# Gate and value projections of a 4-mixer block: two more weight sums on GpSimd, another product order behind the seam, modulation turns moved

## The reference, cut to what matters

```python
def swiglu(u, w1, w3, w2):
    return (jax.nn.silu(u @ w1) * (u @ w3)) @ w2
...
for l in range(DEPTH):                                   # DEPTH = 2
    ada = (c_act @ w_ada[l] + b_ada[l])[:, None, :]
    sh1, sc1, g1, sh2, sc2, g2 = jnp.split(ada, 6, axis=-1)
    u = h * (1.0 + sc1) + sh1
    y = mixer(u, ...)      # ends: (sigmoid(g_a) * y_a + sigmoid(g_b) * y_b) @ w_out
    h = layer_norm(DN_ALPHA * h + g1 * y, ln1_g[l], ln1_b[l])
    u = h * (1.0 + sc2) + sh2
    y = swiglu(u, w1[l], w3[l], w2[l])
    h = layer_norm(DN_ALPHA * h + g2 * y, ln2_g[l], ln2_b[l])
```

## Time and profile before

| | us |
|---|---|
| median of 3 executions | 2423.74 |
| lowest, highest | 2421.90, 2429.11 |
| the profiled execution, its own time | 2421.18 |
| its span in the trace | 2418.9 |
| PE busy | 2304.8 (95%) |
| DVE busy | 1368.0 (57%) |
| ACT busy | 505.8 (21%) |
| POOL busy | 162.6 (7%) |

### The profile page before, as it was taken

The page is one execution under the profiler, slowest core; times in us unless marked ns, Lnnn a source line. Parts: engine busy times, 40 slices in busy tenths (PEclk is TensorE's granted clock), DMA queues, the critical chain, the costliest instruction groups (busy, mean ns, idle before and its releaser), DMA issues.

```text
span 2418.9 us, 29351 instructions
## 1 busy us (share of the span) xinstructions
PE 2304.8 (95%) x11814; PEld 1846.1 (76%) x11814; DVE 1368.0 (57%) x2538; ACT 505.8 (21%) x1088; POOL 162.6 (7%) x133
## 2 busy tenths in 40 slices
PE   7999999899999999988999999999999999888998
PEld 5888587799768876857998655588888874567987
DVE  5764335454647443464767666775566455556666
ACT  1222320110011223101011355322200032432200
POOL 0100001231000000012410000000000000000000
PEclk9999999999999999989999999999999999999999
DMA  9853448454574324564654301433334235234442
GB/s 392 320 209 106 156 167 290 153 179 153 193 279 175 139 105 155 195 246 150 232 187 173 109 35 36 148 106 131 129 122 140 79 136 186 79 114 168 161 159 79
DMA packets 163508, 391.31 MB, mean 162 GB/s; under 512 B 6448, under 2 KB 10928, under 8 KB 160560
## 3 DMA queue, kind: packets, MB, share of 16 engines
q1 hardware_dynamic: 136736, 285.03, 33.0%
q0 software_dynamic: 24080, 93.69, 10.7%
q10 hardware_dynamic: 2560, 10.72, 1.3%
HBM read 388.37 MB, written 1.05 MB: 161 GB/s over the span
## 4 chain that ended last, share of the span: by engine, by line
PE 86%; DVE 6%; DMA 3%; ACT 3%; issue 2%; SPq 0%; DVEq 0%; ACTq 0%
PE bank L523 85%; DMA arena<-in_w_ada 3%; DVE arena L2009 2%; DVE arena L2003 2%; ACT arena L1375 2%; PE bank L521 2%; ACT arena L1378 1%; DVE junk L2009 1%; DVE arena L2006 0%; DVE arena L2923 0%; ACT L1375 0%; DVE arena L2141 0%; DVE arena L2072 0%; DVE arena L2955 0%; SPq L3036 0%
## 5 line engine op out<-in xcount | busy, mean ns | idle before, releaser
L523 PE MATMUL bank<-arena 128*128 128x256 f32 (+3 forms) x11326 | 2247.9, 367 | 71.4 <-DVE arena L2003 23.6
L523 PEld LDWEIGHTS bank<-arena 128*128 128x128 f32 (+1 forms) x11326 | 1788.1, 190 | 518.3 <-issue 296.5
L2003 DVE TENSOR_TENSOR arena<-arena 128x1024 f32<-128x1024 f32 (+9 forms) x555 | 448.1, 821 | 239.2 <-PE bank L523 198.4
L1375 ACT ACTIVATE arena<-arena 128x512 f32<-128x512 f32 (+5 forms) x426 | 213.5, 522 | 822.1 <-DVE arena L2003 452.9
L2009 DVE SCALAR_TENSOR_TENSOR arena<-arena 128x1028 f32<-128x1028 f32 (+6 forms) x367 | 306.1, 850 | 116.9 <-DMA arena<-in_w_ada 82.4
L2003 DVE TENSOR_TENSOR arena<-arena,bank 128x256 f32<-128x256 f32 (+2 forms) x312 | 140.6, 475 | 156.3 <-PE bank L523 148.2
L1378 ACT ACTIVATE arena<-bank 128x512 f32<-128x512 f32 (+1 forms) x207 | 115.3, 595 | 488.0 <-PE bank L523 447.6
L2003 DVE TENSOR_TENSOR arena<-bank,arena 128x512 f32<-128x512 f32 (+3 forms) x103 | 69.7, 690 | 231.4 <-PE bank L523 211.5
L3090 POOL DMA_DIRECT2D arena<-in_w_ada x88 | 62.6, 712 | 1867.6 <-DVEq L2018 1855.4
L1375 ACT ACTIVATE arena<-bank 128x256 f32<-128x256 f32 (+2 forms) x119 | 48.8, 430 | 510.4 <-PE bank L523 509.7
L2009 DVE SCALAR_TENSOR_TENSOR arena<-bank,arena 128x254 f32<-128x254 f32 (+2 forms) x184 | 78.1, 468 | 51.4 <-PE bank L521 35.2
(11 more groups left out here) (33 smaller groups left out, 168.3 us busy)
## 6 DMA issues: line engine op xcount, KB each, us to landing
arena<-in_w_ada POOLq DMA_DIRECT2D x88, 1028.0 KB, 5.5
arena<-in_w_in SPq DMA_DIRECT2D x84, 1024.0 KB, 7.2
arena<-in_w SPq DMA_DIRECT2D x56, 1024.0 KB, 6.4
arena<-in_w_mlp_in SPq DMA_DIRECT2D x32, 1024.0 KB, 6.4
arena<-in_w_mlp_out SPq DMA_DIRECT2D x32, 1024.0 KB, 6.6
arena<-in_w_gla SPq DMA_DIRECT2D x12, 1024.0 KB, 7.3
arena<-in_w_ada SPq DMA_DIRECT2D x16, 514.0 KB, 19.5
arena<-in_w_a SPq DMA_DIRECT2D x8, 1024.0 KB, 7.4
```

Source lines behind the costliest of these rows:

```text
L523: ins = nc.tensor.matmul(out, lhsT, rhs, start=start, stop=stop)
L1375: return nc.scalar.activation(out, x, f, **kw)
L2003: return V.tensor_tensor(out, x, y, op)
```

## The change

All four weight sums of a panel are made by GpSimd, which then waits for products 1 and 2 of the panel; w5 has two places in SBUF by turns (`up_sum`). `first_sum` of the first two panels stands ahead of `up_panel`. Behind the seam PE takes product 1 of both panels after `U 0 0` and product 2 of both after `U 0 1`, turns `U 1 1` ahead of `U 1 0`, and takes product 3 first of the rest of panel 0. In the mix the turns beside `WA 3` and `WB 2` (in layer 1 also the one beside `WA 2`) move behind `mix 3` (three turns in layer 0, two in layer 1) and, in layer 1, two behind panels 1 and 3; the later turns of layer 1 lie behind panels 4, 6, 7, 9. The affine steps move to panels 2, 5 and 8.

```diff
@@ -67,6 +67,8 @@
 HEADS_PER_ADA = 4
 ADA_TAIL = list(range(20, 24))
 ADA_NEXT = list(range(8))
+UP_TURNS = (1, 3, 4, 6, 7, 9)
+UP_AFFINE = (2, 5, 8)
 def layer_panels():
@@ -453,9 +455,19 @@
         up_sums = {i: area(M["QK"] + KH * P * j, KH, P) for j, i in enumerate((5, 6, 7, 4))}
         UP = [(name, p) for p in range(5) for name in ("W1", "W3")]
+        spare_sum = area(M["SIG"] + 1024, KH, 2 * P)
+        def up_sum(at):
+            return spare_sum if at in (1, 3, 5) else down_sum
+        def sum_before(at):
+            return None if at < 2 else at - 2 if at < 7 else at - 1
         def made(l, at, i):
-            return 2 * (l * len(UP) + at) + (1 if i == 5 else 2)
+            return 4 * (l * len(UP) + at) + (5, 7, 6, 3).index(i) + 1
         def up_out(name, p):
@@ -580,9 +592,9 @@
                         ft, tt = 2 * i + j // 2, j % 2
                         mm(ps[:, j * P:j * P + P], H[:, tt, ft * P:ft * P + P], ident, t=True, done=key if j == 3 else None)
-            def tile_transposes(tag, tt):
-                for h in range(2):
+            def tile_transposes(tag, tt, hs=(0, 1)):
+                for h in hs:
                     key = f"{tag} {tt} {h}"
                     ps = open_tile(key)
                     for e in range(4):
@@ -850,16 +862,14 @@
                 def up(name, p, order):
                     q = quarters(first_of[l, "w1"] + 2 * UP.index((name, p)))
-                    ops = {1: (q[0], up_x[0]), 2: (q[1], up_x[2]), 4: (q[3], up_sums[4]), 5: (down_sum, up_sums[5]),
+                    ops = {1: (q[0], up_x[0]), 2: (q[1], up_x[2]), 4: (q[3], up_sums[4]), 5: (up_sum(UP.index((name, p))), up_sums[5]),
                            7: (q[2], up_sums[7]), 6: (q[0], up_sums[6]), 3: (q[1], up_x[3])}
                     for i in order:
                         key = f"{name} {p} {i}"
                         ps = open_tile(key)
                         if i in (4, 5, 6, 7):
                             pe.wait_ge(dve_done, DV.at(f"U x{i}"))
-                        if i in (6, 3):
-                            pe.wait_ge(dve_done, DV.at(f"{name} {p} w{i}"))
-                        if i in (5, 7):
+                        if i in (5, 7, 6, 3):
                             pe.wait_ge(up_sums_made, made(l, UP.index((name, p)), i))
                         for e in range(2):
                             for k in range(KH):
@@ -867,15 +877,17 @@
                                    stop=(k == KH - 1), done=key if e and k == KH - 1 else None)
                 w1, w3 = panel(), panel()
-                drained("U 0 0")
-                drained("U 0 1")
-                for name in ("W1", "W3"):
-                    up(name, 0, FIRST_ORDER[:2])
+                for h in range(2):
+                    drained(f"U 0 {h}")
+                    for name in ("W1", "W3"):
+                        up(name, 0, (h + 1,))
                 pe.wait_ge(dve_done, DV.at("ln1 1"))
-                tile_transposes("U", 1)
-                for name, w in (("W1", w1), ("W3", w3)):
-                    up(name, 0, FIRST_ORDER[2:])
-                    release(w)
+                tile_transposes("U", 1, (1, 0))
+                drained("U 1 1")
+                up("W1", 0, (3, 5, 7, 6, 4))
+                release(w1)
+                up("W3", 0, FIRST_ORDER[2:])
+                release(w3)
                 for name, p in UP[2:]:
                     w = panel()
                     up(name, p, ORDER)
@@ -1592,7 +1604,6 @@
                 act.wait_ge(dve_done, DV.at("cols U"))
                 tile_modulated("U", 0, (0, 1))
                 root_of("ln1", 1)
-                tile_modulated("U", 1, (0,))
                 def first_up(name, p):
@@ -1604,6 +1615,7 @@
                 first_up("W1", 0)
                 first_up("W3", 0)
+                tile_modulated("U", 1, (0,))
                 for p in range(5):
                     for i, m in ((1, 1), (2, 1), (2, 2), (1, 2)):
                         act.wait_ge(dve_done, DV.at(f"W1 {p} c{i}{m}"))
@@ -1611,7 +1623,7 @@
                         func(x, x, ACT.Silu).then_inc(act_done, AC.step(f"gated {p}" if (i, m) == (1, 2) else None))
                     if p:
                         first_up("W3", p)
-                    if p == 3:
+                    if p == 4:
                         act.wait_ge(dve_done, DV.at("h U"))
                         layer_params(l + 1)
                     if p == 0:
@@ -2206,17 +2218,19 @@
                 tt_(c[1, 2], c[1, 2], read(3), ALU.add).then_inc(dve_done, DV.drained(f"{name} 3"))
                 marks[Progress.phase, "dve", f"{name} c12"] = DV.count
+            def up_read(at):
+                key = "{} {}".format(*UP[at])
+                return lambda i: tile(f"{key} {i}")[:, :2 * P].rearrange("p (a b) -> p a b", a=2)
             def up_panel(at):
                 name, p = UP[at]
                 key = f"{name} {p}"
-                n = first_of[l, "w1"] + 2 * at
                 c = up_blocks(name, p)
-                read = lambda i: tile(f"{key} {i}")[:, :2 * P].rearrange("p (a b) -> p a b", a=2)
-                dve.wait_ge(up_sums_made, made(l, at, 7))
-                panel_sums(key, n, 6, f"{key} 1", down_sum)
-                panel_sums(key, n, 3, f"{key} 2", down_sum)
-                first_sum(key, c, read)
+                read = up_read(at)
+                if at > 1:
+                    first_sum(key, c, read)
                 for _ in product_sums(key, c, read):
                     pass
                 if name == "W3":
@@ -2577,7 +2591,7 @@
                         dve.wait_ge(act_done, AC.at(f"GA {j} drained"))
                         tt_(MIX[:, 2 * j:2 * j + 2, :].rearrange("p a b -> p (a b)"), ps[:, :], sg[:, 2 * n, :], ALU.mult).then_inc(
                             dve_done, DV.drained(f"WA {j}"))
-                        beside_mix(1)
+                        beside_mix((1, 1, 1 - l, 0)[j])
                     for n in range(2):
                         j = 2 * p + n
                         dve.wait_ge(pe_done, PE.at(f"WB {j} full"))
@@ -2588,23 +2602,31 @@
                             dve_done, DV.drained(f"WB {j}"))
                         dve.wait_ge(dve_done, DV.count)
                         tt_(x, x, sg[:, 2 * n + 1, :], ALU.add).then_inc(dve_done, DV.step(f"mix {j}"))
-                        beside_mix({0: 1, 1: 5, 2: 1, 3: 1}[j])
+                        beside_mix((1, 5, 0, 3 - l)[j])
                 columns("U", 3)
                 for half in range(2):
                     for tt in range(NT):
                         residual(f"WO {half} {tt}", tt, half, 0)
                         if half:
                             normalise_tile("ln1", tt)
+                first_sum("W1 0", up_blocks("W1", 0), up_read(0))
                 tile_modulated("U", 1, (1,))
                 dve.wait_ge(act_done, AC.at("U 1 0 drained"))
                 token_sums("U", up_x, [up_sums[i] for i in (5, 6, 4)], False, up_sums[7])
+                first_sum("W3 0", up_blocks("W3", 0), up_read(1))
                 for at in range(len(UP)):
                     up_panel(at)
-                    if 2 <= at < 6:
-                        affine_step("U", at - 2)
-                    if l == DEPTH - 1 and at in (2, 4, 6, 8):
-                        ada_turn(7 + at // 2, [("ada", 1), ("adax", 2)])
-                        if at == 8:
+                    if at in UP_AFFINE:
+                        affine_step("U", UP_AFFINE.index(at))
+                        if at == UP_AFFINE[-1]:
+                            affine_step("U", 3)
+                    if l == DEPTH - 1 and at in UP_TURNS:
+                        j = UP_TURNS.index(at)
+                        if j < 2:
+                            beside_mix(1)
+                        else:
+                            ada_turn(6 + j, [("ada", 1), ("adax", 2)])
+                        if j == len(UP_TURNS) - 1:
                             gate("next g1")
                             gate("next g1x")
                     if at == 7:
@@ -3067,24 +3089,30 @@
                 a11, a12, a21, a22 = quarters(n)
                 for m in (n, n + 1):
                     pool.wait_ge(panel_in[m % RING], 16 * (m // RING + 1))
-                if at:
-                    name, p = UP[at - 1]
+                if sum_before(at) is not None:
+                    name, p = UP[sum_before(at)]
                     pool.wait_ge(pe_of[f"layer {l}"], PE.of(f"layer {l}", f"{name} {p} 5 full"))
-                    pool.wait_ge(dve_of[f"layer {l}"], DV.of(f"layer {l}", f"{name} {p} w6"))
                 else:
                     pool.wait_ge(dve_of[f"layer {l}"], DV.of(f"layer {l}", "y_m"))
                     pool.wait_ge(pe_of[f"layer {l}"], PE.of(f"layer {l}", "WA 3 full"))
-                nc.gpsimd.tensor_tensor(down_sum, a21, a22, ALU.add).then_inc(up_sums_made, 1)
```

(12 more changed lines are left out.)

## The result

| | before | after |
|---|---|---|
| median of 5 executions each, same chip | 2425.35 | **2412.9** |
| lowest, highest | 2421.90, 2429.11 | 2410.93, 2415.32 |
| ratio, 95% interval | | 0.9948 [0.9934, 0.9963] |
| the profiled execution, own time | 2421.18 | 2412.96 |
| its span | 2418.9 | 2411.1 |

12.45 us between the medians; 12.8 were forecast, and 2411 as the time. The two profiled executions are 8.2 apart. The changed kernel, timed again beside another 11 runs of before: 2413.87 (2410.91 to 2417.67), ratio 0.9948 [0.9934, 0.9962].

The account below looks back on a forecast made before the run. PE was taken as the bound, one line's matmuls busy 2247.9 of 2418.9 us. Layer 0's -5.6 and layer 1's -7.2 made -12.8, taking 2423.7 to 2411; range 2396 to 2421, the forecast's own 2404 to 2418.

Parts of the forecast that it names:

- The mix's end: End of the mix: without the turn ahead of `WB 3` PE restarts earlier; -0.5 us in layer 0, -12.1 in layer 1.
- The cover: Behind `mix 3` in layer 0: the third turn ends before the third tile's residual is due; 8 us, costed at nothing.
- The seam: Seam, each layer: 10.0 us gained, less 3.5 waiting ahead of product 7 and 1.4 of clock: -5.1, bounds -10.0 and -3.7.
- The panels of layer 1: Layer 1's panels: turns against GpSimd's sums make PE wait 9 us, plus 1.5 of clock: +10, bounds nothing and 19.
- The port: SBUF access: DVE instructions with two SBUF inputs and GpSimd's sums exclude each other, by turns; 3.3 us a pair.
- the first rival: Layer 1's panels: the multiply-accumulate does not exclude GpSimd or wins; +10 falls away, 2401 or 2394; chance 0.32.
- The port costs little: The same as the first rival: turns not slowed by sums, -22.8 for 2401, or -30.0 for 2394; chance 0.32.
- Twice: Layer 1's panels: the port costs twice, +19 for +10, so -3.8 in all, 2420; chance 0.12.
- GpSimd the bound: Ten panels of both layers: a GpSimd sum averages 3.38 us, not 2.35; +13, 2437, slower; chance 0.06.
- The mix's gain absent: After the mix: PE meets the DMAs or the third turn's block is late; 9 us less, -4, 2420; chance 0.05.

Follow-up runs that it names:

- run 9: Kernel before with only `first_sum` of panels 0 and 1 moved behind the token sums, ahead of the first w6 on DVE: 2411.13 us, ratio 0.9934.
- run 11: The changed kernel again, unaltered, timed and profiled beside another 11 runs of before: 2413.87 us, ratio 0.9948.
- run 4: Changed kernel with the products of the six turns in layer 1's panels cut to 8 of 1028 columns: 2402.26 us, ratio 0.9904.
- run 1: Kernel before with only the turns moved; DVE keeps w6 and w3 and the seam stays: 2422.36 us, ratio 0.9992.
- run 2: Changed kernel with the turns put back where they were before: 2409.26 us, ratio 0.9940.
- run 6: Changed kernel with five turns in layer 1's panels (0, 2, 4, 6, 8), the sixth back beside `WA 2`: 2401.36 us, ratio 0.9900.
- run 8: Changed kernel with early w5, w7 of panel 1; in layer 1 from panel 2 DVE makes w6, w3, turn behind next `first_sum`: 2398.06 us, ratio 0.9891.

## Why the prediction was right, step by step

- **The mix's end, -0.5 and -12.1.** Measured -0.5 and -12.1. The cover held: layer 0's third turn waited 5.24 us for its block and no PE wait followed. That the clock would come back held as well: the 64 matmuls of `WO` took 27.73 or 27.74 us behind every wait of 1.51 in these traces. That 1.98 keeps it was less sure than I took it to be (29.43 in run 9). Another -0.5 us ahead of the mix's end in layer 0 was in no term. The worth of the step was another matter, and the end of this section has it.
- **The seam, -5.1 a layer.** Measured -6.8 and -5.3. By its own clock times the waits were to be 1.4, 1.2 (445.5 less 443.3 and 1.04 of transposes) and 3.5, and were 1.42, 1.02 and 3.10; the token sums and GpSimd's went by turns, as read, and x7 did not follow x6 directly. Half of 2.8 us of clock was the cost taken; layer 0 paid nothing, layer 1 1.5, and in run 11 it was the other way round: the half stands for a fall that comes or not.
- **The panels of layer 1, +10.** Measured +13.2 (9.97 of waits, 2.0 clock, 1.2 restarts). The mechanism and its places were right: w6 and w3 late in panels 5 and 6 (0.92, 1.27, 0.41), and the bank late at the third product of panel 9; w3 of panel 8 (1.17) I had only under "smaller ones". The size was not: 6.20 us for the 4.6, which with the clock behind it, 2.0 for 1.5, is 8.2 for 6.1, and the restarts were not in the sum. Two terms were off against each other. A turn was to take 13.2 us with all four products shut out, and took 8.7 to 10.8. But from the end of panel 6 to the awaited add DVE needed 36.2 us for the 33: the waits for sums came to 17.5 for 17.6, none of them lay beside the adds as 2 us were to, and gaps made up the rest; PE, itself held up by 1.17, came after 30.0 for 28.6.
- **The port.** That a multiply-accumulate over SBUF is shut out like a plain one was the assumption against the first rival: 2.90 to 3.26 us for 1.23, 3.3 from start to start forecast, 2.95 to 3.30 measured. By the Trainium skill ("SBUF — State Buffer", Who interferes with whom) a DVE instruction with two SBUF inputs contends with a GpSimd instruction that reads SBUF, and the port pair they share is an exclusive lock; run 4's 8 columns at 2.20 us agree.
- **The rivals.** The port costs little: refuted by those rows. Twice: its +19 is past the 13.2, which lies between it and the +10. GpSimd the bound: a sum took 2.41 to 2.72 us on the mean of its four kinds and layer 0 shows no wait in its panels. The mix's gain absent: it was there in full.

The prediction was right where it counted waits. That the total came so close is in part luck: by layer it had -5.6 and -7.2 for -7.8 and -3.9, the seam was 1.9 us better in the two layers and the panels 3.2 worse, and the clock moves single executions by as much. What it did not ask is whether each part pays for itself. Runs 1 and 2 say that the turns' move does not: 11.8 us at the mix against 13.1 behind it. My sum had the two terms side by side, -12.1 and +10, and laid the second at the door of GpSimd's new sums. In the changed kernel that is what the trace shows; but with DVE making w6 and w3, about 8 of the 13 us come all the same, by another way: the turn stands ahead of w6 in DVE's list (run 1). Short products remove the loss (run 4), so do five turns with a panel between them (run 6), and so does leaving the turns where they were (run 2).

What stays open: what decides whether the clock falls behind a wait of 2 to 3 us, and so some 3 us either way in any one execution; and what makes most executions of the kernel before slower than the profiled one (2421.18, against medians of 2423.89 to 2428.5), which is why run 9 gains 17.4 by the medians and 9.5 between its profiled execution and that of before.

## What to carry to other kernels

Price a moved piece of work where it lands, with everything else that stands there, and time it alone: here the part that looked largest was worth nothing that these runs can tell, and moving two adds ahead of two weight sums was worth the whole change. A wait of PE that ends on nothing the profile names may be a PSUM bank: find the tile eight openings earlier and look when its last reader ran. Where GpSimd is to work beside DVE on SBUF, count each DVE instruction with two operands in SBUF as its own time plus up to nearly one of GpSimd's (here 1.23 plus 2.0), put the GpSimd work where DVE reads PSUM or stands idle, and leave a stretch free behind each heavy block of DVE (run 6). In DVE's own list put such a block behind what PE waits for, not ahead of it (runs 1 and 8).

## What the runs showed of the hardware

- DVE and GpSimd, both with work queued that reads two operands in SBUF, alternate: in layer 1's panels 2.84 to 3.26 us for DVE's 1.23, up to 3.24 for GpSimd's 2.35. With a panel free behind the turn PE lost nothing by it (run 6).
- The size of DVE's instruction hardly matters when it is blocked: 8 columns took up to 2.20 us, 1028 columns took 2.84 to 3.26.
- Equal waits did not leave an equal clock: 1.00 and 0.59 behind 3.10 us in one execution, 0.67 and 1.00 at the same places in another of the same kernel; 7.38 and 8.84 us for the same 64 matmuls behind 2.8 us in two kernels; 27.73 and 29.43 for those behind 1.98.
